# Hybrid decoder step on one core: MoE weight blocks rotated through eight places in reading order, and the sample rows' recurrent work moved behind the first two turned key pages

## The chip, the cores and the metric

The kernel runs on one core of a Trainium2 chip. The metric is the device time of one execution in microseconds (us), lower is better. The engines are PE (TensorE, with its weight loads shown as PEld), DVE (VectorE), ACT (ScalarE), POOL (GpSimd) and SP (SyncE, which here only issues transfers). All data are float32.

## The reference

One layer of a hybrid decoder for 512 prompt rows and 32 sample rows (8 sequences of 4), model width 1024. What matters here, cut from the reference:

```
h = rmsnorm(x);  [hq|hf|hi|hg|mq|mk|mv] = h @ w_in
HGRN2 group (4 heads of 128):  S_t = diag(f_t) S_{t-1} + k_t i_t^T ;  o_t = S_t^T q_t
                               out = rmsnorm_head(o) * silu(hg)
MoBA group (8 heads of 64):    attention over past pages (512 keys for a sample sequence) and the new rows
x += concat(HGRN2 out, MoBA out) @ w_out
x += CrossAttn_4heads(rmsnorm(x), mem K/V)
x += MoE(rmsnorm(x)):  top-1 of 4 groups, top-2 of 8 experts;
     expert(e): hmid = silu(xb @ w1[e]) * (xb @ w3[e]);  return hmid @ w2[e]
y = rmsnorm_final(x)
```

There are 32 experts, each with three 1024x1024 matrices, so 384 MiB of weights are read in the MoE stage. The sample rows have a recurrent state of their own (8 sequences, 4 heads, 128x128), which is read, used for their outputs, updated and written out.

## The kernel before

The program is written engine by engine, with semaphores between them. PE's results go to PSUM banks that are handed out by an ordered list, `plan_jobs`: job n takes bank n modulo 7, and PE waits (`wait_free`) until job n-7 has been emptied by the engine that the list names ("A" for ACT, "V" for DVE). Moving a job in the program needs the same move in the list.

**The sample rows' stage** stands between the prompt's attention and the output projection. On PE it runs: `o` of the sample rows (L2277, L2280: queries times the loaded states `s0`, 65 products), state products `Us` 0 to 3 (L2290), the first page keys turned, `KT` 0 (L2298, 16 transposes), `Us` 4 to 7, `KT` 1, the gated heads turned (`hgT`, L2174), then the first output projection tile `x1` (0,0) (L2088), `KT` 2, scores (L2310), `x1` (0,1), the sample rows' heads turned (L2171), `KT` 3, scores, `x1` (0,2). DVE updates the states from the eight `Us` (L1585, 4 instructions each). POOL loads the states, writes each updated half to HBM, and when a half is out loads the residual input `x_prompt` into the same memory (`r_x`); DVE's first residual add, `add_rows("x1", 0, 0)` (L1630), waits for that load. On DVE, `keys_turned(2)`, `add_rows("x1", 0, 1)` and the sample heads' norm (L1313 to L1515) stand behind this add. SP loads key and value pages when the `KT` and `hgT` jobs are filled.

**The MoE stage.** Each expert's weights are six blocks of 2 MiB: blocks 0 and 1 are the first halves of w1 and w3, 2 and 3 their second halves, 4 and 5 the halves of w2. PE reads them in this order: `up(e)` blocks 0 to 3 (L2643), `down(e-1)` blocks 4 and 5 (L2704), `up(e+1)`, `down(e)` and so on. A loop iteration `pair(j)` handles experts 2j and 2j+1; in the odd expert's `up` the sums of the pair before stand between the blocks (L2658, L2662). Behind `up` come an ACT exponential and a DVE chain (L1977 to L1985), four transposes (L2688) and an ACT copy (L1251); only then `down` may read. Before, a block had a fixed place: six places in `ring`, and two more (`r_h`, `r_mix`) for blocks 0 and 1 of odd experts. SP refills a place when PE's counters `up_used` and `down_used` say that it was read, in a fixed order:

```
            first_weights(0, 2, 0, 2)
            with sp.Fori(1, NE - 3, 2) as e:
                for n in range(2):
                    first_weights(e, n + 2, 1 - n, e + (n + 2))
                    up_weights(e, n + 1, e + (n + 1))
                    down_weights(e, n, e + n, (5, 4) if n else (4, 5))
```

So blocks 0 and 1 of expert e+2 are sent for ahead of blocks 2 and 3 of expert e+1 and of blocks 4 and 5 of expert e.

Of the kernel before, what the change touches and what calls it, by code (L numbers as in the profile page):

```python
# [27 lines left out]
D = 1024  # L28
# [98 lines left out]
def plan_jobs():  # L127
# [63 lines left out]
    add("A", "o", NT)  # L191
# [145 lines left out]
def step_kernel(nc, a):  # L337

    with ExitStack() as ctx:
# [220 lines left out]
        wm_in = [sem(f"moe_w{r}_in") for r in range(6)]  # L560
        wm_odd_in = [sem(f"moe_odd_w{r}_in") for r in range(2)]
        wm_last_in = [sem(f"moe_last_down_w{q}_in") for q in range(2)]
# [50 lines left out]

        def moe_in(r, u):

            return wm_odd_in[r] if u and r < 2 else wm_in[r]


# [16 lines left out]
        def _(sp):  # L635
# [71 lines left out]
            for r in range(2, 6):  # L707
                sp.dma_start(moe_place(r, 0), moe_chunk(r, int(r < 4))).then_inc(wm_in[r], 16)
# [5 lines left out]
            sp.dma_start(moe_place(1, 1), moe_chunk(1, 1)).then_inc(moe_in(1, 1), 16)  # L714

            def slot_of(half):
                J.wait_filled(sp, *last[f"xo{half}"])
                r = WPOS[f"xo{half}"] % 2
                sp.dma_start(moe_place(r, 0), moe_chunk(r, 0)).then_inc(wm_in[r], 16)
# [13 lines left out]
            sp.dma_start(moe_place(0, 1), moe_chunk(0, 1)).then_inc(moe_in(0, 1), 16)  # L733


            def first_weights(b, n, u, expert):
                for r in range(2):
                    sp.wait_ge(up_used, 4 * b + (4 * n + r - 7))
                    sp.dma_start(moe_place(r, u), moe_chunk(r, expert)).then_inc(moe_in(r, u), 16)

            def up_weights(b, n, expert):
                for r in range(2, 4):
                    sp.wait_ge(up_used, 4 * b + (4 * n + r - 3))
                    sp.dma_start(moe_place(r, 0), moe_chunk(r, expert)).then_inc(wm_in[r], 16)

            def down_weights(b, n, expert, parts=(4, 5)):
                for place, r in enumerate(parts):
                    if max(parts[:place + 1]) == r:
# [2043 lines left out]
```

## Time and profile before

| | us |
|---|---|
| median of 3 executions | 1664.52 (1663.5 to 1665.47) |
| profiled execution, its own time | 1666.1 |
| its span | 1664.3 |
| PE busy in the span | 1514.1 (91%) |
| DVE busy | 619.5 (37%) |
| ACT busy | 285.0 (17%) |
| chain that ended last, share of PE | 50% |
| chain that ended last, share of DMA | 40% (38% is `ring<-w`) |

The profiled execution took 1.8 us more than its span, and 1.6 us more than the median. The chain that ended last is followed back from the last instruction; its long DMA share is the MoE weights.

### The profile page before, as it was taken

The numbers are of one execution on the slowest core, as the hardware profiler recorded it, in microseconds if no ns is written. First come the engines' busy times: TensorE is split into PE (matmuls) and PEld (weight loads), VectorE is DVE, ScalarE is ACT, GpSimd is POOL, SyncE is SP. The second block draws the span as 40 slices with busy tenths as digits, with TensorE's granted clock in tenths as the row PEclk, the third lists the DMA queues.
The fourth block names the chain that finished last, engine by engine and source line by source line (L and its number), as shares of the span: only waits on it lengthen the run. The fifth ranks groups of instructions, "written<-read, shape, count | busy, mean of one in ns | idle before, by whom it ended". The sixth has DMA issues, their size and how long they took to land.

```text
span 1664.3 us, 20741 instructions
## 1 busy us (share of the span) xinstructions
PE 1514.1 (91%) x8388; PEld 664.6 (40%) x8388; DVE 619.5 (37%) x1142; ACT 285.0 (17%) x646; POOL 48.3 (3%) x62
## 2 busy tenths in 40 slices
PE   7999999889999989799998989889889998998996
PEld 3544554545444655433333333333233333333332
DVE  2056885353230533632333224233223322423325
ACT  3114335442210321200100000000010000000002
POOL 3000000001010000000000000000000000000000
PEclk9999999999999999899999999999999999999999
DMA  6311220468361278379999999999999999999992
GB/s 224 135 71 51 81 100 14 165 204 325 125 257 51 76 281 329 136 315 428 426 428 429 426 428 427 429 429 428 428 428 427 428 428 428 428 428 428 428 428 92
DMA packets 69643, 500.03 MB, mean 300 GB/s; under 512 B 6912, under 2 KB 7472, under 8 KB 45008
## 3 DMA queue, kind: packets, MB, share of 16 engines
q1 hardware_dynamic: 58704, 468.47, 68.3%
q0 software_dynamic: 7760, 23.92, 4.1%
q10 hardware_dynamic: 3120, 6.82, 1.1%
q8 instruction: 41, 0.67, 0.2%
q14 instruction: 18, 0.15, 0.0%
HBM read 491.97 MB, written 11.14 MB: 302 GB/s over the span
## 4 chain that ended last, share of the span: by engine, by line
PE 50%; DMA 40%; DVE 6%; ACT 2%; issue 1%; SPq 1%; ACTq 0%; DVEq 0%; POOLq 0%
DMA ring<-w 38%; PE psum L2704 11%; PE psum L2088 11%; PE psum L2074 8%; PE psum L2643 4%; PE psum L2183 3%; PE psum L2658 1%; PE psum L2059 1%; DVE ring L1440 1%; PE psum L2433 1%; PE psum L2450 1%; DMA ring<-w_in 1%; PE psum L2231 1%; PE psum L2212 1%; PE psum L2473 1%
## 5 line engine op out<-in xcount | busy, mean ns | idle before, releaser
L2643 PE MATMUL psum<-ring,r_c 128*64 128x512 f32 x1504 | 340.4, 600 | 27.6 <-DMA ring<-w 26.3
L2704 PE MATMUL psum<-ring,r_c 128*64 128x512 f32 x1024 | 238.3, 614 | 54.4 <-DMA ring<-w 40.2
L2643 PEld LDWEIGHTS psum<-ring,r_c 128*64 128x64 f32 x1504 | 110.0, 138 | 250.8 <-issue 190.9
L1959 DVE TENSOR_TENSOR r_x<-r_x,psum 128x1024 f32<-128x1024 f32 x64 | 78.1, 1221 | 268.9 <-PE psum L2658 268.9
L2704 PEld LDWEIGHTS psum<-ring,r_c 128*64 128x64 f32 x1024 | 77.3, 140 | 193.3 <-issue 120.9
L2074 PE MATMUL psum<-r_h,ring 128*128 128x512 f32 x320 | 142.2, 605 | 1.9 <-ACT r_h L879 1.9
L1977 DVE TENSOR_SCALAR r_c<-r_c 128x512 f32<-128x512 f32 x32 | 13.5, 422 | 298.5 <-ACT r_c L1246 298.5
L2658 PE MATMUL psum<-r_c,early 64*128 64x512 f32 x512 | 122.3, 608 | 0.8 <-ACT r_c L1253 0.8
L1246 ACT ACTIVATE r_c<-psum 128x512 f32<-128x512 f32 x32 | 19.1, 598 | 587.9 <-PE psum L2643 587.9
L2088 PE MATMUL psum<-ring,r_h 128*128 128x512 f32 x256 | 113.7, 604 | 1.0 <-DMA ring<-w_in 1.0
L1979 DVE RECIPROCAL r_c<-r_c 128x512 f32<-128x512 f32 x32 | 107.3, 3353 | 1.1
L2074 PEld LDWEIGHTS psum<-r_h,ring 128*128 128x128 f32 x320 | 61.3, 193 | 78.3 <-issue 76.1
L2658 PEld LDWEIGHTS psum<-r_c,early 64*128 64x128 f32 x512 | 46.0, 186 | 76.4 <-issue 76.4
L2088 PEld LDWEIGHTS psum<-ring,r_h 128*128 128x128 f32 x256 | 48.9, 193 | 60.9 <-issue 60.6
L1253 ACT ACTIVATE r_c<-psum 128x512 f32<-128x512 f32 x32 | 19.1, 597 | 265.5 <-PE psum L2704 265.5
L2643 PE MATMUL psum<-r_mix,r_c 128*64 128x512 f32 x256 | 58.4, 598 | 0.0
L2088 PE MATMUL psum<-ring,r_c 128*128 128x512 f32 x128 | 58.2, 600 | 0.0
L2643 PE MATMUL psum<-r_h,r_c 128*64 128x512 f32 x256 | 57.7, 592 | 0.0
L2183 PE MATMUL psum<-ring,r_h 128*128 128x512 f32 x128 | 57.0, 598 | 0.6 <-DVE r_x L1493 0.6
L2088 PE MATMUL psum<-ring,r_mix 128*128 128x512 f32 x128 | 56.8, 597 | 0.8 <-ACT r_mix L879 0.8
L844 POOL DMA_INDIRECT r_c<-tok_rows,table x16 | 17.9, 1119 | 881.7 <-PE psum L2622 774.5
L1630 DVE TENSOR_TENSOR r_x<-r_x,psum 128x512 f32<-128x512 f32 x16 | 11.0, 687 | 74.7 <-PE psum L2088 60.6
(371 smaller groups left out, 1371.1 us busy)
## 6 DMA issues: line engine op xcount, KB each, us to landing
ring<-w SPq DMA_DIRECT2D x158, 2048.0 KB, 23.6
r_mix<-w SPq DMA_DIRECT2D x16, 2048.0 KB, 26.6
r_h<-w SPq DMA_DIRECT2D x16, 2048.0 KB, 27.4
ring<-w_in SPq DMA_DIRECT2D x6, 2048.0 KB, 9.9
ring<-cache_mem_v SPq DMA_DIRECT2D x8, 1024.0 KB, 10.4
ring<-cache_mem_k POOLq DMA_DIRECT2D x8, 1024.0 KB, 7.8
ring<-cache_moba_v SPq DMA_DIRECT2D x24, 256.0 KB, 5.4
ring<-w_xk SPq DMA_DIRECT2D x2, 2048.0 KB, 7.9
```

What stands on the lines that cost most here:

```text
L844: pool.indirect_dma_start(xg, None, tok_rows, bass.IndirectOffsetOnAxis(ap=table[:, c:c + 1], axis=0), bounds_check=TOK - 1, oob_is_err=Fa ...
L1246: act.activation(he[u], psum[2 + 2 * u], ACT.Exp, scale=-1.0).then_inc(up_exp, 1)
L1253: act.activation((late_ys if late else ys)[u], psum[7], ACT.Copy).then_inc(y_free, 1)
L1440: v(dve.reciprocal(g, g))
L1959: return dve.tensor_tensor(x, x, psum_t[:, bank:bank + 2, :].rearrange("p a n -> p (a n)"), ALU.add)
L1979: dve.reciprocal(he[u], he[u]).then_inc(dve_moe, 1)
L2074: ins = pe.matmul(s, w[:, k, P * c:P * (c + 1)], hT[:, k, 0:SEQ], start=(k == 0), stop=(k == KC - 1))
L2088: ins = pe.matmul(J.bank(*name), rows_at(lhs, i)[:, k, :], w[:, k, :], start=(k == 0), stop=(k == KC - 1))
L2183: ins = pe.matmul(J.bank("mem", n, i), memT[:, k, P * i:P * (i + 1)], w[:, k, :], start=(k == 0), stop=(k == KC - 1))
L2643: ins = pe.matmul(psum[2 + 2 * u + m][CAP * half:CAP * (half + 1), :], xT[:, k, CAP * u:CAP * (u + 1)], (first_row(2 + m, kk) if first els ...
L2658: ins = pe.matmul(psum[bank + half], of[e][rr, P * i:P * (i + 1)], src[e][rr, :], start=(e == 0), stop=(e == 1), skip_group_check=True)
L2704: ins = pe.matmul(psum[7][CAP * half:CAP * (half + 1), :], heT[u][:, k % 4, CAP * (k // 4):CAP * (k // 4 + 1)], place[:, kk, 512 * half:51 ...
```

## The change

It has two parts. In the MoE stage all eight places are used in rotation: block number k in PE's reading order goes to place k modulo 8, and SP sends for blocks in just that order. In the sample rows' stage `KT` 0 and `KT` 1 stand first, then the sample rows' `o` and the head transposes, then all eight `Us`; ACT's and DVE's programs and the bank list follow.

```diff
@@ plan_jobs
-    add("A", "o", NT)
-    all_of("V", "Us", range(4))
     keys_turned("KT", 0, "AAAA")
-    all_of("V", "Us", range(4, 8))
     keys_turned("KT", 1)
+    add("A", "o", NT)
     all_of("A", "hgT", range(NT))
+    all_of("V", "Us", range(8))
     add("V", "x1", 0, 0)
@@ places
-        def moe_place(r, u):
-            if u == 0 or r >= 2:
-                return ring[:, 2 * r:2 * r + 2, :, :].rearrange("p a b n -> p (a b) n")
-            return part(r_mix if r else r_h, 0, 4, D)
+        def moe_place(p):
+            if p in (2, 3):
+                return part((r_h, r_mix)[p - 2], 0, 4, D)
+            q = p if p < 2 else p - 2
+            return ring[:, 2 * q:2 * q + 2, :, :].rearrange("p a b n -> p (a b) n")
+        def up_block(e, r):
+            return r if e == 0 else 6 * e - 4 + r
+        def down_block(e, q):
+            return 12 * (NE // 2 - 1) + 8 + q if e == NE - 1 else 6 * e + 6 + q
@@ SP
+            def up_first(b, n):
+                for r in range(2):
+                    p = up_block(n, r) % 8
+                    if n == 2 and isinstance(b, int):
+                        sp.wait_ge(up_used, r + 1)
+                    else:
+                        sp.wait_ge(down_used, 2 * b + (2 * n - 5 + r))
+                    sp.dma_start(moe_place(p), moe_chunk(r, b + n)).then_inc(wm_in[p], 16)
+            def up_second(b, n):
+                for r in range(2, 4):
+                    p = up_block(n, r) % 8
+                    sp.wait_ge(up_used, 4 * b + (4 * n - 5 + r))
...
+            def down_weights(b, n):
+                for q in range(2):
+                    p = down_block(n, q) % 8
+                    sp.wait_ge(up_used, 4 * b + (4 * n + 3 + q))
...
-            first_weights(0, 2, 0, 2)
-            with sp.Fori(1, NE - 3, 2) as e:
...
+            up_first(0, 2)
+            with sp.Fori(0, NE - 7, 4) as e:
+                for n in range(2, 6):
+                    up_second(e, n)
+                    down_weights(e, n - 1)
+                    up_first(e, n + 1)
+            up_second(NE - 4, 2)
+            down_weights(NE - 4, 1)
+            up_first(NE - 4, 3)
+            up_second(NE - 4, 3)
+            down_weights(NE - 4, 2)
             for q in range(2):
-                sp.wait_ge(up_used, 4 * (NE - 2) + q + 1)
-                sp.dma_start(moe_place(q, 0), moe_chunk(4 + q, NE - 1)).then_inc(wm_last_in[q], 16)
+                p = down_block(NE - 1, q) % 8
+                sp.wait_ge(down_used, 2 * (NE - 3) + q + 1)
+                sp.dma_start(moe_place(p), moe_chunk(4 + q, NE - 1)).then_inc(wm_in[p], 16)
@@ ACT: head_squares(NT) and its root move from ahead of the xv_prompt output to here
             keys_turned(0)
             keys_turned(1)
+            head_squares(NT)
+            J.wait_emptied(act, "o", NT)
+            act.activation(hy0[:, NT, 0:1], hss[:, NT, 0:1], ACT.Abs_reciprocal_sqrt, ...)
             for i in range(NT):
                 turn_heads(i)
@@ DVE
             heads_normed()
-            gate_applied(NT)
...
-            for n in range(4):
-                sample_states(n)
-            for n in range(4, 8):
+            keys_turned(1)
+            gate_applied(NT)
+            for n in range(8):
                 sample_states(n)
-            keys_turned(1)
             dve.wait_ge(xr_in[0], 16)
             add_rows("x1", 0, 0)
@@ PE
-            sample_states(range(4))
             keys_turned(0)
-            sample_states(range(4, 8))
             keys_turned(1)
+            sample_heads_out()
             for i in range(NT):
                 turn_heads(i)
+            sample_states(range(8))
@@ PE, the loop over pairs is unrolled by two so that places are constants
-            with pe.Fori(1, NE // 2 - 1) as j:
-                pair(j)
+            with pe.Fori(1, NE // 2 - 2, 2) as b:
+                for at in range(2):
+                    pair(b, at)
```

SP's transfers at the end of the MoE stage, before the change, behind the loop: blocks 0, 1 of expert 31; 2, 3 of 30; 4, 5 of 29; 2, 3 of 31; 4, 5 of 30; 4, 5 of 31.

```order
L739 DMA r_h<-w 128x4096 [waits moe_up_weights_used]
L739 DMA r_mix<-w 128x4096 [waits moe_up_weights_used]
L744 DMA ring<-w 128x4096 [waits moe_up_weights_used] x2
L750 DMA ring<-w 128x4096 [waits moe_down_weights_used] x2
L744 DMA ring<-w 128x4096 [waits moe_up_weights_used] x2
L750 DMA ring<-w 128x4096 [waits moe_down_weights_used] x2
L765 DMA ring<-w 128x4096 [waits moe_up_weights_used] x2
```

The same place of the changed kernel, with the tensors told apart (w1, w3, w2), behind its loop: 2, 3 of expert 30; 4, 5 of 29; 0, 1 of 31; 2, 3 of 31; 4, 5 of 30; 4, 5 of 31.

```order
L756 DMA r_h<-w1 128x4096
L756 DMA r_mix<-w3 128x4096
L763 DMA ring<-w2 128x4096 x2
L750 DMA ring<-w1 128x4096
L750 DMA ring<-w3 128x4096
L756 DMA ring<-w1 128x4096
L756 DMA ring<-w3 128x4096
L763 DMA r_h<-w2 128x4096
L763 DMA r_mix<-w2 128x4096
L779 DMA ring<-w2 128x4096 x2
```

The two blocks for `up` of expert 31 moved from ahead of four other blocks to behind them; the last six blocks are the same in both.

PE in the sample rows' stage, before, from the sample rows' `o` (`atts` and `s0` in `r_x`) on:

```order
L2277 MATMUL psum<-ring,atts 128x128
L2280 MATMUL psum<-r_x,r_mix 32x128 x32
L2290 MATMUL psum<-r_c,ring 128x512 x4
L2298 MATMUL psum<-ident,r_h 128x128 x16
L2290 MATMUL psum<-r_c,ring 128x512 x4
L2298 MATMUL psum<-ident,r_c 128x128 x16
L2174 MATMUL psum<-ident,ring 128x128 x16
L2088 MATMUL psum<-ring,r_mix 128x512 x8
L2298 MATMUL psum<-ident,ring 128x128 x16
L2310 MATMUL psum<-ring 32x512 x8
L2088 MATMUL psum<-ring,r_mix 128x512 x8
L2171 MATMUL psum<-ident,ring 128x128
```

The same engine and place in the changed kernel:

```order
L2311 MATMUL psum<-ident,r_h 128x128 x16
L2311 MATMUL psum<-ident,r_c 128x128 x16
L2290 MATMUL psum<-ring,atts 128x128
L2293 MATMUL psum<-r_x,r_mix 32x128 x32
L2186 MATMUL psum<-ident,ring 128x128 x16
L2303 MATMUL psum<-r_c,ring 128x512 x8
L2100 MATMUL psum<-ring,r_mix 128x512 x8
L2311 MATMUL psum<-ident,ring 128x128 x16
L2323 MATMUL psum<-ring 32x512 x8
L2100 MATMUL psum<-ring,r_mix 128x512 x8
L2183 MATMUL psum<-ident,ring 128x128
```

The two groups of 16 key transposes now stand ahead of the products that read the loaded state; what follows from `x1` (0,0) on is in the old order. The instructions are the same in number.

## Rows read from the trace of the kernel before

**Rows 1.** The page: transfer rate in 40 slices of 41.6 us.
```profile
GB/s 224 135 71 51 81 100 14 165 204 325 125 257 51 76 281 329 136 315 428 426 428 429 426 428 427 429 429 428 428 428 427 428 428 428 428 428 428 428 428 92
```
**Rows 2.** Windows: busy PE, PEld, DVE, ACT, POOL, then granted clock, DMA share, GB/s.
```profile
740.00:760.00 20.00, 18.76 (x94) 7.05 (x92) 6.70 (x7) 2.82 (x7) 1.18 (x1) 1.00 1.00 427
868.00:888.00 20.00, 15.95 (x74) 5.23 (x72) 5.15 (x4) 1.19 (x2) 0.00 (x0) 1.00 1.01 432
1000.00:1200.00 200.00, 179.54 (x936) 64.54 (x938) 63.98 (x67) 14.88 (x32) 3.30 (x3) 1.00 1.01 428
```
**Rows 3.** Timeline of PE, end of MoE: start, us, instructions, [idle before <-releaser].
```profile
1571.38 8.78 PE L2704 MATMUL psum<-ring,r_c 128*64 128x512 f32 x32 [1.91 <-DMA ring<-w]
...
1590.86 3.65 PE L2643 MATMUL psum<-ring,r_c 128*64 128x512 f32 x16 [0.40 <-DMA ring<-w]
...
1600.65 3.65 PE L2704 MATMUL psum<-ring,r_c 128*64 128x512 f32 x16 [1.11 <-DMA ring<-w]
1604.13 3.60 PE L2643 MATMUL psum<-r_h,r_c 128*64 128x512 f32 x16
1607.66 1.99 PE L2658 MATMUL psum<-r_c,early 64*128 64x512 f32 x8
...
1622.90 3.65 PE L2643 MATMUL psum<-ring,r_c 128*64 128x512 f32 x16
...
1627.92 7.09 PE L2704 MATMUL psum<-ring,r_c 128*64 128x512 f32 x32 [0.69 <-ACT r_c L1251]
...
1636.38 7.09 PE L2704 MATMUL psum<-ring,r_c 128*64 128x512 f32 x32 [0.69 <-ACT r_c L1251]
```
**Rows 4.** The line of the `down` products: ns of one, shortest, median, longest.
```profile
L2704 PE MATMUL psum<-ring,r_c x1024: 592/592/1116, 746.2 to 1642.9; 128*64 128x512 f32 x171
```
**Rows 5.** Timeline of DVE, end of the gate chain of expert 31.
```profile
1631.80 0.69 DVE L1985 TENSOR_TENSOR r_c<-r_c,psum 128x512 f32<-128x512 f32 x1
```
**Rows 6.** The page: transfers of MoE weights, KB each, median us to landing.
```profile
ring<-w SPq DMA_DIRECT2D x158, 2048.0 KB, 23.6
```
**Rows 7.** Timeline of PE, sample rows' stage.
```profile
365.21 0.77 PE L2277 MATMUL psum<-ring,atts 128*128 128x128 f32 x2 [4.91 <-issue]
365.90 3.64 PE L2280 MATMUL psum<-r_x,r_mix 128*32 128x128 f32 x64
...
370.92 1.97 PE L2298 MATMUL psum<-ident,r_h 128*128 128x128 f32 x16
...
381.37 7.10 PE L2088 MATMUL psum<-ring,r_mix 128*128 128x512 f32 x16 [0.78 <-ACT r_mix L879]
...
392.00 7.13 PE L2088 MATMUL psum<-ring,r_mix 128*128 128x512 f32 x16
400.70 0.33 PE L2171 MATMUL psum<-ident,ring 128*128 128x128 f32 x1 [1.56 <-DVE ring L1515]
...
405.78 7.13 PE L2088 MATMUL psum<-ring,r_mix 128*128 128x512 f32 x16
```
**Rows 8.** Timeline of DVE, sample rows' stage.
```profile
371.02 8.35 DVE L1585 SCALAR_TENSOR_TENSOR r_x<-r_x,dl,psum 128x128 f32<-128x128 f32 x32 [1.12 <-PE psum L2290]
...
394.34 0.69 DVE L1630 TENSOR_TENSOR r_x<-r_x,psum 128x512 f32<-128x512 f32 x1 [13.76 <-DMA r_x<-x_prompt]
394.94 1.28 DVE L1309 COPY ring<-psum 128x512 f32<-128x512 f32 x2
```
**Rows 9.** Timeline of POOL, its transfers in the sample rows' stage.
```profile
375.54 1.18 POOL L810 DMA_DIRECT2D hg_sample<-r_x  x1 [19.76 <-DVE r_x L1585]
...
383.74 0.71 POOL L813 DMA_DIRECT2D r_x<-x_prompt  x1 [2.91 <-DMA hg_sample<-r_x]
```
**Rows 10.** Windows of 1 us, columns as in rows 2.
```profile
363.00:364.00 1.00, 0.00 (x0) 0.00 (x0) 0.97 (x3) 0.00 (x0) 0.00 (x0) 0.73 1.00 283
...
370.00:371.00 1.00, 1.00 (x9) 0.08 (x2) 0.00 (x0) 0.57 (x3) 0.00 (x0) 0.86 1.05 387
```

More of the change, by code:

```diff
@@ L2272, in _, with sample_heads_out @@
                     heads_out(p)
[L2273 to L2282 removed]
+            def sample_heads_out():
+                J.wait_free(pe, "o", NT)
+                pe.wait_ge(s0_in, 16)
+                pe.wait_ge(qkx_done, 1)
+                s = J.bank("o", NT)
+                pe.matmul(s[:, 0:HD], atts[:, :], vhs, start=True, stop=False, skip_group_check=True)
+                for b in range(NB):
+                    for h in range(HG):
+                        ins = pe.matmul(s[NS * h:NS * (h + 1), 0:HD], qx[:, h, NS * b:NS * (b + 1)], s0[:, b, h, :],
+                                        start=False, stop=(b == NB - 1), skip_group_check=True)
+                J.fills(ins, "o", NT)
             def sample_states(numbers):
@@ L2623, in rows_turned, with up @@
                 ins.then_inc(xt_full, 1)
-            def up(j, c, inside={}):
-                u = c % 2
+            def up(b, at, c, inside={}, late=False):
+                j, u = b + at if at else b, c % 2
                 if c == 0:
@@ L2679, in pieces, with down @@
                 return {0: these(0, 1), 1: these(2), 2: these(3, 4)}
-            def down(j, c, last=False, late=False):
-                u = c % 2
+            def down(b, at, c, late=False):
+                j, u = b + at if at else b, c % 2
                 first = isinstance(j, int) and 2 * j + c == 0
@@ L2705, in down, with pair @@
                                             heT[u][:, k % 4, CAP * (k // 4):CAP * (k // 4 + 1)],
-                                            place[:, kk, 512 * half:512 * (half + 1)],
+                                            moe_place(place)[:, kk, 512 * half:512 * (half + 1)],
                                             start=(k == 0), stop=(k == KC - 1), skip_group_check=True)
                     ins.then_inc(down_used, 1)
-            def pair(j):
-                up(j, 0)
-                down(j, -1)
-                up(j, 1, pieces(j))
+            def pair(b, at):
+                j = b + at if at else b
+                up(b, at, 0)
+                down(b, at, -1)
+                up(b, at, 1, pieces(j))
                 pe.wait_ge(sum_free, 5 * j - 1)
@@ L2716, in pair @@
                 pe.wait_ge(sum_free, 5 * j)
-                down(j, 0)
+                down(b, at, 0)
             def slot_tables():
@@ L2743, in _ @@
             n_ov = pe.value_load(ovi[0:1, 0:1], min_val=0, max_val=XBLK)
-            up(j, 0)
-            down(j, -1)
-            up(j, 1, pieces(j))
+            up(j, 0, 0)
+            down(j, 0, -1)
+            up(j, 0, 1, pieces(j))
             pe.wait_ge(sum_free, 5 * j)
-            down(j, 0)
-            down(j, 1, last=True)
+            down(j, 0, 0)
+            down(j, 0, 1)
             with pe.If(n_ov > 0):
@@ L2754, in _ @@
                         for u in range(2):
-                            up(j, u)
-                            down(j, u, late=True)
+                            up(j, 0, u, late=True)
+                            down(j, 0, u, late=True)
                         pe.wait_ge(late_sel_made, 2 * j - (NE - 2))
```

89 lines of the change are left out of this document (31 added, 58 removed).

## The prediction

> **What bounds the kernel now.** I read the page's rate line first: from the nineteenth slice on it stands at 426 to 429 GB/s and doesn't move [rows 1]. In windows the MoE stage shows a DMA share of 1.00 to 1.01 from 740 us on, while PE is busy for 179.5 of 200 us [rows 2]. A block of 2 MiB at 428 GB/s takes 2.097/0.428 = **4.90 us**; PE reads one in 3.65 us (16 recorded products), so it waits. The timeline says the same: the reads that waited for a transfer start at 1590.86 and 1600.65, two blocks apart in SP's order, 9.79 us [rows 3]. In this stage a faster PE or another order buys nothing; only three things can: an earlier start of the full stream, fewer idle transfer engines within it (none are seen), and less PE work behind its end.
>
> The third is there. The last read that waited for a transfer is block 5 of expert 29 at 1600.65 [rows 3]. From then on PE runs without such a wait: four blocks of `up(31)` with the sums between them, the last from 1622.90, `down(30)` from 1627.92, `down(31)` from 1636.38 to 1643.47. Yet after block 5 of expert 29 only six blocks are still to land, so the last is there at about 1600.6 + 6 x 4.90 = 1630, and PE reads it 10 us later. The stage ends on PE, which started its last stretch too late, not on the stream.
>
> Ahead of the MoE stage the chain is mostly PE. In the sample rows' stage PE stands idle for 4.91 us until the recurrent states are loaded, and again for 1.56 us before it turns the sample heads at 400.70 [rows 7]. The second wait is DVE's: it stood 13.76 us waiting for the residual input, until 394.34 [rows 8].
>
> **The rotation: the end of the stage.** It removes and adds no work; SP sends for the same 192 blocks, and the waits come at the same points of PE's reading (up(0), up(1), then each `down` and `up` as it is read). So the stream should stay full, and its end moves only with its start. What changes is which block arrives when. Before, the order behind the loop is 0,1 of expert 31; 2,3 of 30; 4,5 of 29; after it is 2,3 of 30; 4,5 of 29; 0,1 of 31. The last six blocks are the same. Counted back from 1630, block 5 of expert 29 now lands at about 1590.8 and block 0 of expert 31 at 1595.7, block 1 at 1600.6, and `up(31)`'s last two at 1605.5 and 1610.4.
>
> I follow PE with the old durations. Block 5 of expert 29 is read from 1590.8 to 1594.4, block 0 of expert 31 from 1595.7. In the old profile that block started at 1604.13, and from there to the end of `down(31)` at 1643.47 no transfer was waited for: 39.3 us. Does one stand in the way now? After the start at 1595.7, the old distances put the last `up` block at 1595.7 + (1622.90 - 1604.13) = 1614.5 (landed 1610.4), `down(30)` at 1619.5 with its second block at 1623 (landed 1620), `down(31)` at 1628.0 with its second block at 1631.5 (landed 1630). DVE's gate chain of expert 31 ended at 1632.49, some 6 us behind the last `up` product [rows 5], so 1624 now, ahead of need. No transfer stands in the way, and the end moves from 1643.47 to 1595.7 + 39.3 = 1635.0: **-8.5 us**. It is one interval of the stream (4.90) plus one block read (3.65) that no longer lies ahead of `up(31)`. The bounds: no more than 1643.5 - (1630 + 3.65) = 9.8 us, since the last block must land and be read; and less where PE's clock falls. A `down` whose clock had fallen took 8.78 instead of 7.09 us [rows 3], and one product 1116 instead of 592 ns, which makes 6.9 us of a block [rows 4]: 1.7 to 3.2 us lost, so at least 5.3 us stay.
>
> **Within the stage** PE now waits some 1.25 us at nearly every block, where before it had two blocks of four in store. From 868 to 888 us it already ran so, a wait at each of four blocks, 15.95 of 20 us busy, and the granted clock was 1.00 [rows 2]. I cost this at nothing; its cover is 58.8 - 52.8 = 6 us of PE's slack in a pair of experts. The Trainium skill ("TensorE: Matmul & The Clock Gate", section "HAM oscillation — how this bites in real kernels") tells of a kernel that falls to the low clock at each tile because it waits for transfers between short runs of products; by it the even reads could all become slow. Its waits were longer than its runs, the ones here are a third of them; the trace so far speaks against it, and it stands below as a rival.
>
> Blocks will be in the queue for longer: 23.6 us from issue to landing now [rows 6]; with seven places sent for ahead of the one being read, up to 7 x 4.90 = 34 us. [...]
>
> **The sample rows' stage.** The two key groups (1.97 us for 16 transposes [rows 7]) fit into PE's wait of 4.91 us, their pages having been sent for long before. The state's products can start no earlier than now, 365.2; I allow 0.3 us for the `xv_prompt` output, which ACT now issues ahead, 365.5. But PE's clock had fallen in that wait (0.73 at 363) and came back at 370 [rows 10], so the 65 products took 4.3 us; at the full clock they take about half (592 against 1116 ns for a product [rows 4]), and are done at 367.7 instead of 369.5. The 16 head transposes take 2.0 us like the keys', then the state products: DVE's updates (8.35 us from 371.02 [rows 8]) start at about 370.1. `x1` (0,0) follows at 372.3 (it needs the bank of the second `Us`), instead of 381.37, and with `KT` 2 and the scores at the old 10.6 us distance `x1` (0,1) starts at 382.9 and ends at 390.0, instead of 399.1. **Nine us earlier, but not kept:** next PE turns the sample heads, and they stand on DVE behind the residual input. That load is issued when the written half of the states is out: write at 375.54, load at 383.74 [rows 9], data at 394.34, 18.8 us of queues that are full in both. DVE is 0.9 us earlier, so the data come at about 393.4. Behind it DVE needs 0.6 + 1.28 for the add and two key copies and 1.5 for the second add and the norm, so PE goes on at 396.8 instead of 400.70: 3.9 us. It has then been idle for 6.8 us, and the clock is down; after the earlier such wait it took 5 us of work to come back. The transposes of that time (0.33 + 1.97 at full clock) take twice as long and the scores part of it: about 1.9 us of the 3.9 are lost, and `x1` (0,2) starts near 403.8 instead of 405.78. **-2.0 us** at the start of all that follows, which hangs on PE; the MoE stream starts and ends that much earlier. Bounds: where the clock doesn't fall, -3.9; where the load comes 3 us later, +1.
>
> That is not excluded: key pages 3 and 4 and value pages 0 and 1 now go out 4 to 8 us earlier, into the time of the state's write and the load, whereas `xv_prompt`'s output leaves it. All queues together moved about 390 GB/s then (387 at 370 us [rows 10]). The Trainium skill ("DMA: Bandwidth & Descriptors", section "Issuing engines are not separate DMA queues") has transfers of all issuing engines interleave on the same 16 engines, which would put each earlier page in part ahead of the load. One page group is 1 MiB, 2.7 us at that rate. I take no net delay, because the same pages were ahead of the load before; only key page 5, sent for behind `KT` 2 at 381 instead of 390, is new there.
>
> **Sum.** 1666.1 - 8.5 - 2.0 = 1655.6 for the profiled execution; the median stood 1.6 below it, so **1654.0**.
>
> **The rivals.**
> 1. Only the end's gain: the residual load comes later through the earlier pages, or the fallen clock takes the whole gain. For it: DVE's 13.76 us there. Term +1 to 0: 1656.5 (1655.5 to 1657.5).
> 2. The end's gain is cut by a low clock in `up(31)` or `down`: 5.3 instead of 8.5, 1657.2. For it: the `down` of 8.78 us; against it: sums fill the waits of `up(31)`.
> 3. Both larger: clock kept and load early, end at its bound: -3.9 - 9.8, 1651.
> 4. The rotation changes nothing at the end, because PE is late for reasons of its own (gate chain, sums); the gain is the 2 us alone, 1662.5. Against it: the start at 1604.13 hangs directly on the transfer at 1600.65.
> 5. Slower: the clock falls at the many waits. A block then takes 6.9 us, 3.2 more, against a slack of 6 us in a pair; two such blocks in a pair are free, a third costs 3 x 3.2 - 6 = 3.6 us in each of 15 pairs, 54 us: about 1708. It decides from the third block on. Against it: 868 to 888 us.
>
> **How the numbers follow.** Forecast (gains of 9 to 12) 0.55, rival 1 0.17, 2 0.10, 3 0.06, 4 0.08, 5 0.04. The range 1650.8 to 1659.3 takes in the forecast, 1, 2 and most of 3 and leaves out some 0.15. A measurement of this kernel tells a change from none at about 0.2%, 3.3 us. Faster: all but 4 and 5, and a little less: 0.88. Same 0.07 (most of 4 lies at -2.0 us). Slower 0.05.
>
> **What the profile after would show.** Right: DMA share 1.0 to within 35 us of the last product; the weights' landing time near 30 us or more; DMA waits at the first two blocks of each `up`; the block ahead of `up(31)` read some 5 us before it; `down(31)` over within 6 us of the last landing. In the sample stage: no PE wait near 361, a wait of 5 to 8 us for DVE at 390, clock 0.50 behind it. Wrong: a rate under 426 GB/s or gaps in the stream; clock 0.5 in even `up` reads; the residual input later than 395.

## The result and the profile after

The changed kernel takes **1654.52 us** at the median (1651.67 to 1655.87, five runs), against 1664.52 us (1663.5 to 1665.47) of the kernel before on the same chip. The ratio is 0.9932, 95% interval 0.9919 to 0.9945: faster by 0.7%, 10.0 us. The forecast was 1654.0.

The profiled execution took 1651.67 us with a span of 1649.9. It is the fastest of the five, and 14.4 us under the profiled execution of before, where the medians stand 10.0 apart. So its parts are read one by one, and each is held against a second profile of the same changed kernel (the run e11_after_again below).

Four marks cut the program: the start of the sample rows' `o`, the end of their stage (the 32 small products of the new rows' scores, 0.4 us ahead of `x1` (0,2)), the third group of products of `up(0)`, and the last sums of the MoE stage. Windows between these marks, columns as in [rows 2]; the kernel before:

```profile
0.00:365.21 365.21, 335.98 (x2056) 173.63 (x2056) 190.01 (x407) 128.10 (x311) 15.44 (x26) 0.99 0.32 109
405.36:719.16 313.80, 290.62 (x1719) 160.66 (x1712) 111.23 (x354) 66.12 (x143) 12.22 (x16) 0.95 0.50 185
719.16:1644.25 925.09, 843.54 (x4330) 305.87 (x4327) 288.85 (x308) 72.82 (x157) 16.38 (x15) 0.99 0.98 417
```

The changed kernel, the same windows:

```profile
0.00:364.59 364.59, 339.08 (x2087) 176.85 (x2088) 189.92 (x407) 130.41 (x317) 15.45 (x26) 1.00 0.32 109
403.29:712.62 309.33, 286.39 (x1718) 159.67 (x1712) 111.27 (x354) 66.12 (x143) 12.22 (x16) 0.97 0.51 188
712.62:1629.82 917.20, 836.85 (x4330) 293.75 (x4327) 288.94 (x308) 72.73 (x157) 16.41 (x15) 1.00 0.99 420
```

And the changed kernel in its second profile:

```profile
0.00:367.77 367.77, 342.19 (x2087) 178.41 (x2088) 189.93 (x407) 130.51 (x317) 15.44 (x26) 0.99 0.32 108
406.26:718.47 312.21, 287.73 (x1719) 160.43 (x1713) 111.28 (x354) 66.17 (x143) 12.27 (x16) 0.96 0.51 186
718.47:1635.90 917.43, 836.88 (x4330) 293.80 (x4327) 288.92 (x308) 72.83 (x157) 16.39 (x15) 1.00 0.99 420
```

The MoE stage is 7.9 us shorter in the first profile (925.09 - 917.20) and 7.7 in the second. The sample rows' stage takes 38.70 us (364.59 to 403.29) and 38.49, against 40.15 before (365.21 to 405.36): 1.5 and 1.7 us less. But 40.15 is the shortest of the five profiles that have the old order of this stage: e1, e3 and e8 below took 41.19 each and e12 took 41.04, since there the second group of 16 key transposes fell to the low clock (3.2 to 3.35 us instead of 1.97). The new order took 38.3 to 38.7 us in all six profiles that have it unaltered on PE. So it is worth 1.5 to 2.9 us. The rest of the 14.4 us doesn't belong to the change: the stretch between the two stages took 309.33 us in one profile of the changed kernel and 312.21 in the other, with the same instructions and a granted clock of 0.97 and 0.96, and all the other profiles, whatever the kernel, have 312.1 us or more there. The stretch ahead of both took 364.59 and 367.77.

**The end of the MoE stage.** Timeline of PE after the change; it answers to [rows 3]:

```profile
1574.87 3.65 PE L2661 MATMUL psum<-r_mix,r_c 128*64 128x512 f32 x16 [1.24 <-DMA r_mix<-w]
...
1579.89 3.65 PE L2720 MATMUL psum<-ring,r_c 128*64 128x512 f32 x16 [0.69 <-ACT r_c L1265]
1584.66 3.65 PE L2720 MATMUL psum<-ring,r_c 128*64 128x512 f32 x16 [1.11 <-DMA ring<-w]
1589.65 3.65 PE L2661 MATMUL psum<-ring,r_c 128*64 128x512 f32 x16 [1.34 <-DMA ring<-w]
...
1621.95 7.09 PE L2720 MATMUL psum<-ring,r_c 128*64 128x512 f32 x32 [0.69 <-ACT r_c L1265]
1629.82 7.14 PE L2676 MATMUL psum<-r_c,early 64*128 64x512 f32 x32 [0.79 <-ACT r_c L1267]
```

The reader should see the distances between block reads: 1574.87, 1579.89, 1584.66, 1589.65 are about 4.9 us apart, one stream interval each. Block 5 of expert 29 is read at 1584.66 and block 0 of expert 31 follows at 1589.65 as soon as it has landed. From there to the end of `down(31)` (1621.95 + 7.09 = 1629.04) PE waits for no transfer: 39.4 us, where the prediction had 39.3.

The wait view of the changed kernel for 807 to 1600 us (total, times, longest) shows how the waiting was spread:

```profile
PE psum L2720 <- ACT r_c L1265: 26.2, 27, 1.2
PE psum L2661 <- DMA ring<-w: 17.3, 16, 1.3
PE psum L2720 <- DMA ring<-w: 12.2, 12, 1.1
PE psum L2661 <- DMA r_h<-w: 11.9, 11, 1.3
PE psum L2661 <- DMA r_mix<-w: 7.4, 6, 1.2
```

PE's lines for the same groups in the kernel before:

```profile
PE psum L2704 <- DMA ring<-w: 39.1, 26, 1.9
PE psum L2643 <- DMA ring<-w: 26.3, 22, 1.9
PE psum L2704 <- ACT r_c L1251: 9.6, 14, 0.7
```

The sum is 75.0 us in both: PE waits as long as before, in 72 pieces instead of 62. None of these waits of PE is longer than 1.3 us in the changed kernel; before, 1.9 us were common. With that the slow `down` products are gone. The line of these products, which answers to [rows 4], has no product above 644 ns now; the page's line of the ring's weights answers to [rows 6]:

```profile
L2720 PE MATMUL psum<-ring,r_c x768: 592/592/644, 739.7 to 1628.4; 128*64 128x512 f32 x192
```
```profile
ring<-w SPq DMA_DIRECT2D x142, 2048.0 KB, 33.3
```

**The sample rows' stage.** PE after the change, which answers to [rows 7]:

```profile
364.59 0.46 PE L2290 MATMUL psum<-ring,atts 128*128 128x128 f32 x2 [1.09 <-ACT ring L893]
364.98 1.95 PE L2293 MATMUL psum<-r_x,r_mix 128*32 128x128 f32 x64
...
382.86 7.13 PE L2100 MATMUL psum<-ring,r_mix 128*128 128x512 f32 x16
397.28 0.47 PE L2183 MATMUL psum<-ident,ring 128*128 128x128 f32 x1 [7.29 <-DVE ring L1529]
397.55 3.15 PE L2311 MATMUL psum<-ident,r_h 128*128 128x128 f32 x16
```

DVE, which answers to [rows 8]:

```profile
369.92 8.36 DVE L1598 SCALAR_TENSOR_TENSOR r_x<-r_x,dl,psum 128x128 f32<-128x128 f32 x32 [2.63 <-PE psum L2303]
393.97 0.69 DVE L1643 TENSOR_TENSOR r_x<-r_x,psum 128x512 f32<-128x512 f32 x1 [15.69 <-DMA r_x<-x_prompt]
```

POOL, which answers to [rows 9]:

```profile
374.44 1.18 POOL L824 DMA_DIRECT2D hg_sample<-r_x  x1 [19.10 <-DVE r_x L1598]
...
385.43 0.71 POOL L827 DMA_DIRECT2D r_x<-x_prompt  x1 [5.70 <-DMA hg_sample<-r_x]
```

The wait for the states is filled; the 64 products take 1.95 us instead of 3.64; `x1` (0,1) starts at 382.86 instead of 392.00. Then PE stands still for 7.29 us: DVE has the residual input at 393.97 instead of 394.34. The transposes behind the wait take 3.15 us; the granted clock is 0.50 from 397 to 400 us.

### The profile page after: what moved, and what is told of

It reads as the page before. It is cut to its first block, busy times and chain, and to the rows that moved or that the text cites. A ratio compares the mean times of both kernels' runs of the same rounds, so it can differ in the third digit from the quotient of the medians.

```text
span 1649.9 us, 20691 instructions
## 1 busy us (share of the span) xinstructions
PE 1500.6 (91%) x8388; PEld 651.2 (39%) x8388; DVE 619.7 (38%) x1142; ACT 284.1 (17%) x646; POOL 48.4 (3%) x62
## 4 chain that ended last, share of the span: by engine, by line
PE 64%; DMA 25%; DVE 6%; ACT 4%; issue 1%; SPq 0%; ACTq 0%; DVEq 0%; POOLq 0%
PE psum L2661 17%; DMA ring<-w 11%; DMA r_h<-w 11%; PE psum L2100 10%; PE psum L2086 8%; PE psum L2676 7%; PE psum L2720 6%; PE psum L2195 3%; PE psum L2635 1%; PE psum L2071 1%; ACT r_c L1252 1%; DVE ring L1454 1%; PE psum L2446 1%; PE psum L2463 1%; ACT ring L893 1%
## 5 line engine op out<-in xcount | busy, mean ns | idle before, releaser
L2661 PE MATMUL psum<-ring,r_c 128*64 128x512 f32 x1504 | 339.4, 598 | 18.5 <-DMA ring<-w 17.3
L2720 PE MATMUL psum<-ring,r_c 128*64 128x512 f32 x768 | 172.7, 597 | 33.7 <-ACT r_c L1265 21.4
L2661 PEld LDWEIGHTS psum<-ring,r_c 128*64 128x64 f32 x1504 | 104.6, 137 | 240.6 <-issue 218.6
L1260 ACT ACTIVATE r_c<-psum 128x512 f32<-128x512 f32 x32 | 19.1, 597 | 599.0 <-PE psum L2661 599.0
L2720 PEld LDWEIGHTS psum<-ring,r_c 128*64 128x64 f32 x768 | 52.2, 137 | 137.6 <-issue 89.8
L1267 ACT ACTIVATE r_c<-psum 128x512 f32<-128x512 f32 x32 | 19.1, 597 | 245.4 <-PE psum L2720 245.4
## 6 DMA issues: line engine op xcount, KB each, us to landing
ring<-w SPq DMA_DIRECT2D x142, 2048.0 KB, 33.3
```

The source lines that it names most:

```text
L1260: act.activation(he[u], psum[2 + 2 * u], ACT.Exp, scale=-1.0).then_inc(up_exp, 1)
L1267: act.activation((late_ys if late else ys)[u], psum[7], ACT.Copy).then_inc(y_free, 1)
L2661: ins = pe.matmul(psum[2 + 2 * u + m][CAP * half:CAP * (half + 1), :], xT[:, k, CAP * u:CAP * (u + 1)], (first_row(2 + m, kk) if first els ...
L2720: ins = pe.matmul(psum[7][CAP * half:CAP * (half + 1), :], heT[u][:, k % 4, CAP * (k // 4):CAP * (k // 4 + 1)], moe_place(place)[:, kk, 51 ...
```

## The experiments

Sets that ran on one chip share its runs of the kernel before, whose medians were 1666.05 us (e1 to e4), 1667.17 (e5 to e7), 1666.52 (e8 to e11) and 1666.09 (e12). Kernels of different sets are compared by their ratios to it, in square brackets the 95% interval. My theory was the prediction's: the end's gain comes from the place of `up(31)`'s blocks among the last transfers, the small rest from the sample stage, where the residual load takes the larger gain back.

**The two halves apart.** e1 is the changed kernel with the sample rows' stage of before; e2 is the kernel before with that stage alone changed.

> The rotation of the eight places alone, with the sample rows' stage as before. My theory: the whole gain at the end of the stage and nothing at its start, -8.5 us against the kernel before (ratio 0.9949); the start of up(31) hangs on its own first block and not on block 5 of expert 29. Rival (the end's gain is not the order but comes from the earlier start only): no difference, ratio 1.000. Rival (the change in the sample stage does more than 2 us and the rotation less): -5 us or less.

> The new order of the sample rows' stage alone, with the weight places and SP's order as before. My theory: -2 us (ratio 0.9988), PE waiting some 7 us for DVE at about 390 and at the half clock behind it, and up to some 4 us more or less by the time at which the clock comes back at three later places. Rival (the order is worth the 4 to 6 us more that the profiled execution of the changed kernel shows ahead of the MoE stage): -6 us, ratio 0.996.

e1: 1658.55 us, 0.9951 [0.9931, 0.9971]; its MoE stage between the marks took 917.12 us. e2: 1664.26 us, 0.9992 [0.9975, 1.001], stage 924.98, and its sample stage 38.54 us. The shorter MoE stage is the rotation's. The other half's 1.5 to 2.9 us are seen in each profile that has it, and are too small for the time of a whole run to tell.

**One line of the order, in either direction.** e3 takes the kernel before and moves the first two blocks of expert 31 back; e4 takes the changed kernel and moves them forward.

```diff
# e3, on before
-            first_weights(0, NE - 1, 1, NE - 1)
             up_weights(0, NE - 2, NE - 2)
             down_weights(0, NE - 3, NE - 3)
+            first_weights(0, NE - 1, 1, NE - 1)
# e4, on the changed kernel
             up_second(NE - 4, 2)
-            down_weights(NE - 4, 1)
             up_first(NE - 4, 3)
+            down_weights(NE - 4, 1)
```

> The kernel before with one line moved: blocks 0 and 1 of expert 31 are sent for behind blocks 2, 3 of expert 30 and 4, 5 of 29, ahead of the last six; all places and the loop as before. My theory: the end's gain is a matter of this one order, so -8.5 us (ratio 0.9949), as in the rotation alone. Rival (it takes the deeper queue or the even waits of the rotation through the whole stage): less than 2 us.

> The changed kernel with one pair swapped: blocks 0 and 1 of expert 31 are sent for ahead of blocks 4 and 5 of expert 29. Block 5 of expert 29 then lands two intervals later, where it did before the change, so my theory gives the end's gain back: +8.5 us against the changed kernel, -2 to -3 us against the kernel before (ratio 0.998 to 0.999). Rival (the order of these blocks is not the cause): as the changed kernel, ratio 0.993.

e4: 1664.78 us, 0.9995 [0.9978, 1.0013], stage 927.10: the whole gain of the end is gone by one exchanged pair. Its PE timeline shows where:

```profile
1593.23 9.95 PE L2720 MATMUL psum<-ring,r_c 128*64 128x512 f32 x32 [10.44 <-DMA ring<-w]
```

`down(29)` waits 10.44 us, since two blocks of expert 31 land ahead of its own, loses the clock (9.95 instead of 7.09 us), and all of `up(31)` is left behind it. Of the 9.9 us given back, the order itself accounts for 7.0 and the fallen clock for 2.9.

e3: 1663.62 us, 0.9987 [0.9969, 1.0006], stage 923.06. That was a miss: this line brings only 2.0 of the 7.9 us. Its PE timeline:

```profile
1570.72 8.78 PE L2704 MATMUL psum<-ring,r_c 128*64 128x512 f32 x32 [1.89 <-DMA ring<-w]
1579.30 13.93 PE L2643 MATMUL psum<-ring,r_c 128*64 128x512 f32 x64
...
1633.76 7.09 PE L2704 MATMUL psum<-ring,r_c 128*64 128x512 f32 x32 [0.69 <-ACT r_c L1251]
```

The last wait for a transfer is at `down(28)` now, not at `down(29)`. In the order of before, the first two blocks of *every* expert go ahead of four others, those of expert 30 too. So `down(28)` starts at 1570.72 with both blocks of `up(30)` already there, and from then on PE has 70 us of work of its own. Of these, 1.7 us are a fallen clock (8.78 for 7.09 us in `down(28)`), which here lies on the path; with the clock kept the line would have brought 3.7 us. Moving the last expert's blocks alone uncovers the same fault one expert earlier. My theory had the end right and its cause too narrow: the reading order must hold for more than the last expert. For how many it must hold was not tested.

**The order without the rotation of places.** If the order alone does it, the eight places may stay where they were. e8 sends in the changed kernel's order with the fixed places of before, its loop starting with expert 2:

```diff
-            first_weights(0, 2, 0, 2)
-            with sp.Fori(1, NE - 3, 2) as e:
+            with sp.Fori(0, NE - 3, 2) as e:
                 for n in range(2):
-                    first_weights(e, n + 2, 1 - n, e + (n + 2))
-                    up_weights(e, n + 1, e + (n + 1))
-                    down_weights(e, n, e + n, (5, 4) if n else (4, 5))
...
+                    first_weights(e, n + 2, n, e + (n + 2))
+                    up_weights(e, n + 2, e + (n + 2))
+                    down_weights(e, n + 1, e + (n + 1))
```

> The kernel before with its fixed places, but with SP's order through the whole stage that of PE's reading: 0 and 1, 2 and 3 of expert e, then 4 and 5 of e-1. The line moved at the end alone had given only -2 us, since PE was then without a wait from down(28) on and bound by its own work. My theory now: it is the order over the last two pairs that counts and not the rotation of places; from the third block of the first up to the last sums the kernel before takes 925.1 us and the five with the rotation 917.1 to 917.4, and this one should take 917 to 918, -8 us in all (0.995). Rival (with fixed places SP must wait for down(e-1) to be read before it sends blocks 4, 5 of e, so the stream runs dry now and then, as once in the run with the one line moved): the gain is smaller or gone, up to 15 us slower.

e8: 1667.47 us, 1.0004 [0.9985, 1.0023], stage 924.17. As a total, no gain; but the windows say that the end was gained and the start lost. A window of e8 at the start of the stream:

```profile
735.00:755.00 20.00, 18.77 (x94) 7.07 (x92) 11.90 (x12) 2.22 (x6) 1.18 (x1) 1.00 0.59 231
```

The same of the kernel before:

```profile
735.00:755.00 20.00, 18.76 (x94) 7.17 (x92) 9.67 (x10) 2.82 (x7) 1.18 (x1) 1.00 0.99 419
```

e8's transfer engines are busy for 0.59 of this window. Counted from each kernel's own mark, e8 moved 37.0 MB in the first 100 us of the stage (205, 361, 430 GB/s in its first three fifths and 427 in the rest), the kernel before 40.0 and the changed kernel 40.1: 3.1 MB less than the latter are 7.2 us of the stream, and e8's stage is 7.0 us longer than the changed kernel's. SP sent nothing between 722.0 and 742.36: it stood at the wait for the places that `up(1)`'s second pair still held, while those of its first pair, `r_h` and `r_mix`, came free ahead of them (before, SP filled these at 733.22 and 736.49). Its last part has the form of the changed kernel's (each block read as it lands, then 39.4 us without such a wait). e12 keeps the end and mends the start with the old order for experts 2 and 3:

```diff
             first_weights(0, 2, 0, 2)
-            with sp.Fori(1, NE - 3, 2) as e:
+            first_weights(0, 3, 1, 3)
+            up_weights(0, 2, 2)
+            down_weights(0, 1, 1)
+            up_weights(0, 3, 3)
+            down_weights(0, 2, 2)
+            with sp.Fori(2, NE - 3, 2) as e:
                 for n in range(2):
...
```

> The kernel before with its fixed places and SP's order that of PE's reading from expert 4 on; only at the start blocks 0 and 1 of expert 3 are sent for ahead of 2, 3 of expert 2 and 4, 5 of expert 1, as before the change. In the run with the reading order throughout and fixed places, the end had the new form (39.4 us from the first block of up(31) to the last of down(31)), but the stream stood nearly still from 730 to 745 us and the stage took 924.2 us. My theory: that gap comes from the two free places of expert 3 that SP did not fill until down(0) was read, and is all that fixed places cost; with them filled the stage takes 917 to 918 us, -8 us in all (ratio 0.995). Rival (fixed places cost something in every pair, or the gap only moves): 920 to 925 us, ratio 0.997 to 1.000.

e12: 1659.98 us (1658.34 to 1665.19), 0.9955 [0.994, 0.9971], with the sample stage of before; e1, the rotation alone, had 0.9951. Its MoE stage is 1643.32 - 723.93 = 919.4 us, against 925.1 before and 917.1 to 917.4 with rotation: between the 917 to 918 of my theory and the 920 to 925 of the rival. PE at its end:

```profile
1603.15 3.65 PE L2643 MATMUL psum<-r_h,r_c 128*64 128x512 f32 x16 [1.34 <-DMA r_h<-w]
...
1635.45 7.09 PE L2704 MATMUL psum<-ring,r_c 128*64 128x512 f32 x32 [0.69 <-ACT r_c L1251]
```

The same 39.4 us from the last awaited block to the end of `down(31)`. The missing 2 us lie in the first 100 us of the stream, in two windows of e12 that begin 40 and 60 us behind the mark:

```profile
763.93:783.93 20.00, 19.31 (x92) 6.62 (x90) 5.16 (x4) 1.77 (x3) 0.00 (x0) 1.00 1.00 411
783.93:823.93 40.00, 38.76 (x212) 13.92 (x210) 13.15 (x15) 2.83 (x7) 1.16 (x1) 1.00 1.00 417
```

The changed kernel at the same distances:

```profile
752.62:772.62 20.00, 19.31 (x92) 6.63 (x90) 5.16 (x4) 1.77 (x3) 0.00 (x0) 1.00 1.01 432
772.62:812.62 40.00, 38.77 (x212) 13.93 (x210) 13.15 (x15) 2.82 (x7) 1.16 (x1) 1.00 1.00 425
```

21 GB/s over 20 us and 8 over 40 are 0.74 MB, 1.7 us of the stream. Three other profiles of the rotation (e1, e9, e11) have 429 to 431 GB/s in the first window and 424 to 426 in the second. Why the rate is lower in e12 isn't shown. So the order alone gives the end's gain. The rotation of places isn't what gains it; it allows that order from the first block on, with no free place left idle.

**Who delays the residual load.** The chain from the write of the states (POOL's issue) to the residual data at DVE took 18.80 us before and 19.53 after. The other profiles make the difference clearer: 17.7 to 18.3 us in the four others with the old order of this stage (e1, e3, e8, e12), 19.2 to 19.3 in the three others with the new one (e2, e4, e11). The rival to "a chain of fixed length" was that the pages sent ahead of it share its engines. e5 sends the first two value pages only when the load is in; e9 holds back everything from key page 3 on:

```diff
# e5
-            J.wait_filled(sp, "hgT", NT - 1)
-            value_pages(0, 1)
             for b in (5, 6, 7):
                 J.wait_filled(sp, "KT", b - 3, 3)
                 key_pages(b)
+                if b == 5:
+                    sp.wait_ge(xr_in[0], 16)
+                    value_pages(0, 1)
# e9
             J.wait_filled(sp, "KT", 0, 3)
+            sp.wait_ge(xr_in[0], 16)
             key_pages(3)
```

> The changed kernel, with SP's value pages 0 and 1 (2 MiB) sent for only when the first half of the residual input has landed, behind key page 5. In the changed kernel's profile the states' first half took 10.7 us to be written and the load 8.5 us behind it, and PE waited 7.3 us. My theory: the write and the load share the transfer engines with the pages that now go out earlier, so without these two the residual input lands some 5 to 8 us earlier, PE's wait at 390 shrinks to under 2 us and the clock isn't lost: -6 to -9 us against the changed kernel (ratio against the kernel before 0.988 to 0.990). Rival (the load's time is its own queue's, write, receipt and load one after the other, whatever else runs): no difference against the changed kernel, 0.993.

> The changed kernel, with key pages 3 and 4 and value pages 0 and 1 (4 MiB, all that SP sends for between 369 and 383 us) held until the first half of the residual input has landed. From the issue of the states' first write to the landing of the load it took 18.8 us before the change, 19.5 after it, and 18.9 without the two value pages. Theory A (the write and the load share the engines with whatever SP has queued): now under 14 us, PE's wait of 7.3 us is gone and the clock isn't lost; -5 us or more against the changed kernel, less what the later key pages cost. Theory B (the chain is bound by POOL's own queue: two writes of 512-byte rows and the load behind them): again 18 to 20 us, and the late key page 3 adds up to 3 us: ratio 0.993 to 0.996 against the kernel before.

e5: 1656.45 us, 0.9932 [0.9916, 0.9948]; its chain took 18.90 us (377.46 to 396.36). A miss: two groups of pages less shorten the chain by 0.3 to 0.6 us only (19.2 to 19.5 in the profiles of the same order). My reading is that value page 2 and key pages 3 and 4 fill the queue all the same: the windows from 380 to 395 us still show 393 to 403 GB/s. e9: 1656.67 us, 0.9932 [0.9909, 0.9955], beside 0.9941 [0.9919, 0.9962] for the changed kernel in the same set. Here the chain is shorter, 375.00 to 389.46 = 14.46 us, while all queues together moved 283 GB/s from 374 to 380 us and 246 from 380 to 386 (388 and 391 in the changed kernel). DVE of e9:

```profile
389.46 0.69 DVE L1644 TENSOR_TENSOR r_x<-r_x,psum 128x512 f32<-128x512 f32 x1 [10.62 <-DMA r_x<-x_prompt]
```

PE of e9 behind it:

```profile
392.78 0.33 PE L2184 MATMUL psum<-ident,ring 128*128 128x128 f32 x1 [2.22 <-DVE ring L1530]
395.69 3.68 PE L2312 MATMUL psum<-ident,r_h 128*128 128x128 f32 x16 [2.58 <-DMA r_h<-cache_moba_k]
```

The pages do take their share: 5.1 us of 19.5. But the page that was held back is itself needed right behind the wait; PE waits 2.58 us for it and runs at the low clock. The stage took 38.47 us, as without it. So the sharing that I expected is there and the gain of 5 us isn't.

**State products ahead of the heads.** The sample rows' state updates can start the chain earlier when PE turns the heads behind them; e6 does that alone, e7 with e5's edit, e10 with e9's:

```diff
-    all_of("A", "hgT", range(NT))
     all_of("V", "Us", range(8))
+    all_of("A", "hgT", range(NT))
...
             sample_heads_out()
+            sample_states(range(8))
             for i in range(NT):
                 turn_heads(i)
-            sample_states(range(8))
```

> The changed kernel with the eight state products ahead of the four head transposes on PE. DVE's updates then start about 2 us earlier, and with them the write and the residual load; PE's wait shrinks from 7.3 to some 3 to 4 us, at the edge of losing the clock. My theory (what follows hangs on the chain update, write, load, add): -2 us, and up to -4 where the clock stays. Rival (the transfers are the bound and a write sent for earlier only waits longer): 0.

> Both of the last two edits. Theory: PE is then bound by its own work in this stage, so no better than the value pages sent late alone by more than 1 us: ratio 0.987 to 0.990. Rival (both only shift the same wait): as the changed kernel, 0.993.

> The same with the state products ahead of the head transposes, which gave -1.5 us beside the changed kernel, and -4 with the value pages late. Theory A: PE is bound by its own work, ratio 0.989 or less. Theory B: 0.992 to 0.995.

> The changed kernel once more, for its profile. Its first profiled execution was 14.4 us faster than that of before, though the medians are 10.0 apart; I put some 4 us of it to the times at which PE's clock came back at three places (482, 612 and 706 us), which vary between executions. If so, this one has the same 917.2 us from the third block of up(0) to the last sums and about 38.7 us in the sample rows' stage, but 311 to 316 us between the two instead of 309.3, and 8 to 13 us less in all than the kernel before. Rival (the change gains something there): 309 to 310 us again.

e6: 1653.97 us, 0.9924 [0.9908, 0.994], sample stage 36.67 us. e7: **1650.83 us** (1647.36 to 1651.97), **0.9896 [0.988, 0.9912]**, stage 34.82. e10: 1651.43 us, 0.9919 [0.989, 0.9949], stage 34.23. e11, the changed kernel again: 1658.1 us, 0.9941 [0.9919, 0.9962]; its middle stretch took 312.21 us, as expected, and its profiled time is 7.5 us under that of the kernel before, just outside the 8 to 13 expected. PE of e6:

```profile
375.64 9.13 PE L2100 MATMUL psum<-ring,r_mix 128*128 128x512 f32 x16 [0.73 <-ACT r_mix L893]
...
397.00 0.33 PE L2183 MATMUL psum<-ident,ring 128*128 128x128 f32 x1 [1.56 <-DVE ring L1529]
397.16 1.91 PE L2311 MATMUL psum<-ident,r_h 128*128 128x128 f32 x16
```

DVE of e6, its second residual add:

```profile
395.47 0.69 DVE L1643 TENSOR_TENSOR r_x<-r_x,psum 128x512 f32<-128x512 f32 x1 [1.54 <-PE psum L2100]
```

PE of e7:

```profile
375.50 7.10 PE L2101 MATMUL psum<-ring,r_mix 128*128 128x512 f32 x16 [0.73 <-ACT r_mix L894]
...
395.47 0.33 PE L2184 MATMUL psum<-ident,ring 128*128 128x128 f32 x1 [2.20 <-DVE ring L1530]
395.64 1.91 PE L2312 MATMUL psum<-ident,r_h 128*128 128x128 f32 x16
```

Counted from the start of `o`, the write of the states goes out 1.9 us earlier in both, and the data are there 2.3 (e6) and 2.5 us (e7) earlier than in the changed kernel. The heads stand ahead of `x1` (0,0) as before, but now each group of them waits for DVE to empty a bank (0.27 and three times 0.41 us in e7, and 0.73 for ACT), so PE comes to its long wait 2.6 us later in e7. The wait of 7.29 us thus shrinks from both ends to 2.20, the clock is kept behind it (1.91 us for the 16 transposes, 3.15 in the changed kernel), and the stage is 3.9 us shorter: 2.5 from the earlier data and 1.4 from the clock.

e6 is another case. Its clock fell at 373 us, with the same instructions of PE and nearly the same waits as e7 up to there; `x1` (0,0) took 9.13 us, and `x1` (0,1) came so late that DVE waited 1.54 us for it with the residual data already there. Its wait of 1.56 us is the time of DVE's second add and norm and has nothing to do with the load. In e10 it is the same: 1.56 us, DVE having waited 2.78 us for PE. So in e10 PE is bound by its own work and the shorter chain of 15.39 us brings little more, 34.23 us against 34.82. That PE would be bound by its own work was theory A of e10; the ratio of 0.989 or less that went with it isn't borne out.

e7 has the lowest ratio. Its interval lies wholly below both those of the changed kernel, and overlaps those of e6 and e10. Its expectation held in the number (0.987 to 0.990), not in the reason: I had the late value pages as the larger part, and alone they bring nothing. Between the ratios of e7 and of the changed kernel lie 6 us or more, of which the stage shows 3.9; the rest is not explained.

## Why the prediction was right, point by point

- **The end, -8.5 us.** 7.9 and 7.7 were measured. The path was as worked out: last awaited block, then 39.4 us (39.3 foreseen), with no transfer in the way. Of the remaining 0.6 to 0.8 us, 0.4 are that block 5 of expert 29 was read 9.45 us earlier, counted from the start mark of the stage, and not 9.85; why stays open. The *reason* given, the two blocks no longer ahead of `up(31)`, was too narrow: by e3 it brings 2.0 us, 3.7 with the clock kept, and the rest comes with the reading order of the experts before. The sum came out right since it was made from the changed kernel's whole order of arrival and not from the difference of two lines.
- **The waits within the stage, at nothing.** Right: clock 1.00, waits of 1.1 to 1.3 us at most blocks. The rival of 1708 us fell. The case of the Trainium skill ("TensorE: Matmul & The Clock Gate", section "HAM oscillation — how this bites in real kernels") has waits for transfers that are longer than the runs of products between them. This stage has none such, 1.3 us at most beside reads of 3.65, so its even reads don't test the page. What moved was the opposite: the slow products of before, 8.78 us for a `down` [rows 3], vanished with the 1.9 us waits. This was not in the sum, and costs nothing as long as a later wait for the stream takes it up, as behind all five of them before.
- **Landing time** "up to 34": 33.3 us, with the stream at 420 GB/s over the whole stage.
- **The sample stage, -2.0 us.** The stage gave 1.5 and 1.7, and 2.3 to 2.9 against the other profiles of the old order. Products done at 366.9 (367.7 foreseen), updates at 369.9 (370.1), `x1` (0,1) at 382.9 (382.9), data at 394.0 (393.4), PE again at 397.3 (396.8), wait 7.3 us (6.8), clock lost, and `x1` (0,2) at 403.7 (403.8). A step that was off is "no net delay": the chain became longer, by 0.7 us in the pair of profiles and by 0.9 to 1.6 between the others. And the reading of the second wait *before* the change was wrong. The prediction put PE's 1.56 us at 400.70 down to the residual input at 394.34. But DVE's second add, which the sample heads' norm stands behind, waited for PE's own `x1` (0,1):

```profile
399.18 0.69 DVE L1630 TENSOR_TENSOR r_x<-r_x,psum 128x512 f32<-128x512 f32 x1 [2.95 <-PE psum L2088]
```

The load had 2.95 us to spare there. It came onto the path only because the change made PE faster ahead of it. The sum isn't hurt, since it follows the changed kernel from the data on, and gets PE's restart right to 0.5 us. The bound "-3.9 where the clock doesn't fall" was not reached by the change. e7 goes beyond it (34.82 us, 5.3 less than before), but with data that come earlier too.
- **The page rule that spoke for a late load** (the Trainium skill, "DMA: Bandwidth & Descriptors", section "Issuing engines are not separate DMA queues", transfers of all issuers share the same 16 engines): the runs agree. With the pages held back the chain took 14.5 us instead of 19.5 (e9), and 15.4 instead of 19.1 (e10 and e6). Before and after alike ran beside such pages, at 367 to 408 GB/s in all, so the change moved the chain by about 1 us only.
- **From profile to median.** I took 1.6 us as their distance. The profiled execution was 2.9 us below its median this time, and in the second set 0.5 above it. The forecast of that execution was 1655.6 and it took 1651.67, 3.9 us less. That 1654.0 agrees with 1654.52 to half a microsecond is luck: no term is that well known, and the second set puts the same kernel at 0.9941 instead of 0.9932.

## What to carry to other kernels

At the end of a stage that a stream bounds, count what the engine still has to do behind the last block it had to wait for. That is set by the order of arrival over more than the last unit; send in the order of reading, but never at the price of a free place that stands idle behind a wait, as at the start in e8. A stretch made faster beside a transfer chain can bring the chain onto the path, lengthen the wait at its end and lose the clock there. Start the chain earlier: let the engine first do what the chain waits for, and only then work that nobody waits for. And read off which engine ended a wait last, in the old kernel as in the new one.

## What the runs showed of the hardware

The clock can fall in one execution and not in another at the same place with the same instructions: `x1` (0,0) took 9.13 us in e6 and 7.10 in e7, behind waits of 0.3 to 0.7 us in both. The stretch from 406 to 719 us varies too: fourteen profiles of kernels with the same code there took between 309.3 us (granted clock 0.97) and 316.2 (0.95). That spread of 7 us is nearly as large as the end's gain, so a single pair of profiles can't be read as a total: 14.4 us showed where 10.0 are real. And reads of 3.65 us with a wait of 1.1 to 1.3 us between kept the full clock for 900 us, while of the 13 `down` products ahead of which PE had waited 1.9 us in the kernel before, 5 ran at a fallen clock (8.78 for 7.09 us; granted 0.50 from 1572 to 1575 us).
